# A down projection with its operands changed over: tokens held, weights moving

## The reference, cut to what matters

```python
    h2 = rmsnorm(x, g_norm[1]) * (1 + sc2) + sh2
    u, gg = jnp.split(h2 @ w_ffn_in, 2, axis=-1)          # 1024 -> 2 x 2816
    x = x + gt2 * ((jax.nn.silu(gg) * u) @ w_ffn_out)     # 2816 -> 1024
    ...
    y_prompt = rmsnorm(xp, g_final)
    y_sample = rmsnorm(xs, g_final)
```

## Time and profile before

| | |
|---|---|
| median of 3 runs | 1036.57 us (1036.42 to 1037.43) |
| span of the profiled execution | 1034.1 us (its own time is not given apart from this; the median is 2.5 above it) |
| TensorE busy | 995.1 us, 96% |
| TensorE's weight loads busy | 914.6 us, 88% |
| VectorE, ScalarE, GpSimd busy | 521.6, 447.0, 359.7 us |
| first matmul of the down projection | 884.79 us after the span's start |

### The profile page before, as it was taken

One profiled execution on the slowest core, in us unless ns is written; L12 is line 12 of the kernel. 1 busy time (PEld: TensorE's weight loads), 2 busy tenths in 40 slices (PEclk: granted clock), 3 DMA queues, 4 the chain that ended last, 5 costly groups with the idle time before them and its releaser, 6 DMA issues.

```text
span 1034.1 us, 26814 instructions
## 1 busy us (share of the span) xinstructions
PE 995.1 (96%) x10988; PEld 914.6 (88%) x10988; DVE 521.6 (50%) x1200; ACT 447.0 (43%) x991; POOL 359.7 (35%) x318
## 2 busy tenths in 40 slices
PE   6999999999999989998899999999999999999996
PEld 4899999899998666776788999999999999999996
DVE  4500000078006666666547756888888887800003
ACT  4433323354345444554432355555555556711113
POOL 1164344342332433600252354333233342133330
PEclk9999999999999999999999999999999999999998
DMA  9986756334412000002332632232423323232212
GB/s 356 395 299 228 247 189 212 107 126 148 137 45 60 13 14 13 14 24 76 126 98 85 204 122 82 74 90 82 121 81 95 108 81 97 60 110 85 84 57 87
DMA packets 118182, 122.33 MB, mean 118 GB/s; under 512 B 5396, under 2 KB 102848, under 8 KB 115656
## 3 DMA queue, kind: packets, MB, share of 16 engines
q1 hardware_dynamic: 112864, 111.86, 33.2%
q10 hardware_dynamic: 5224, 9.10, 2.7%
HBM read 108.33 MB, written 15.23 MB: 119 GB/s over the span
## 4 chain that ended last, share of the span: by engine, by line
PE 85%; DVE 7%; ACT 4%; issue 2%; POOL 1%; ACTq 1%; DVEq 0%; POOLq 0%
PE ps L1964 60%; PE ps L2586 21%; PE ps L2328 1%; DVE s_sb L1542 1%; PE ps L2228 1%; DVE hl L1356 1%; DVE Pb L1513 1%; ACT x_sq L871 0%; POOL w_lo L685 0%; DVE XX L1523 0%; PE ps L2619 0%; POOL w_lo L839 0%; ACTq L857 0%; DVE rbx L1369 0%; PE ps L2115 0%
## 5 line engine op out<-in xcount | busy, mean ns | idle before, releaser
L1964 PE MATMUL ps<-hh,w_hi 128*128 128x274 f32 x832 | 176.1, 294 | 1.5 <-DVE hl L1356 0.7
L685 POOL TENSOR_TENSOR w_lo<-w_raw,w_hi 128x2048 fp32r<-128x2048 f32 x22 | 101.4, 4607 | 213.9 <-ACT w_hi L881 197.2
L1964 PE MATMUL ps<-hl,w_hi 128*128 128x274 f32 x832 | 172.9, 290 | 1.0 <-DVE al L1878 1.0
L1964 PE MATMUL ps<-hh,w_lo 128*128 128x274 f32 x832 | 173.2, 290 | 0.0
L1964 PEld LDWEIGHTS ps<-hh,w_hi 128*128 128x128 f32 x832 | 131.5, 189 | 11.7 <-issue 9.9
L1964 PEld LDWEIGHTS ps<-hl,w_hi 128*128 128x128 f32 x832 | 131.5, 189 | 1.2 <-DVE al L1878 1.2
L1964 PEld LDWEIGHTS ps<-hh,w_lo 128*128 128x128 f32 x832 | 131.6, 190 | 0.8 <-issue 0.8
L833 POOL TENSOR_TENSOR ws_lo<-w_raw,ws_hi 128x512 fp32r<-128x512 f32 x63 | 80.6, 1294 | 144.8 <-DVE ps L1796 130.3
L2586 PE MATMUL ps<-th,ws_hi 128*128 128x274 f32 x336 | 97.5, 290 | 0.0
L2586 PE MATMUL ps<-tl,ws_hi 128*128 128x274 f32 x336 | 97.4, 290 | 0.0
L2586 PE MATMUL ps<-th,ws_lo 128*128 128x274 f32 x336 | 97.1, 289 | 0.0
(11 more groups left out here) (438 smaller groups left out, 2288.0 us busy)
## 6 DMA issues: line engine op xcount, KB each, us to landing
w_raw<-in_w_ffn_in SPq DMA_DIRECT2D x44, 512.0 KB, 4.5
w_raw<-in_w_in SPq DMA_DIRECT2D x42, 512.0 KB, 5.0
ada_l<-in_w_ada SPq DMA_DIRECT2D x16, 1024.0 KB, 6.6
ada_w<-in_w_ada SPq DMA_DIRECT2D x8, 1024.0 KB, 13.4
w_raw<-in_w_ffn_out SPq DMA_DIRECT2D x16, 384.0 KB, 3.9
w_raw<-in_w_ffn_out SPq DMA_DIRECT2D x16, 320.0 KB, 3.2
g_d<-gst SPq DMA_DIRECT2D x16, 274.0 KB, 2.2
gring<-g_d SPq DMA_DIRECT2D x16, 274.0 KB, 3.2
```

What stands on the lines that cost most here:

```text
L685: pool.tensor_tensor(w_lo[:, s, 0:cols], w_raw[:, s, 0:cols], w_hi[:, s, 0:cols].bitcast(F32), ALU.subtract).then_inc(lo_done, 1)
L1964: return pe.matmul(out, lhsT, rhs, start=start, stop=stop)
```

## The change

The down projection changes its operands over. What is held in the array is now a 128x128 block of activations (128 tokens of one channel block), and 512 columns of `w_ffn_out` move past it. The result comes out with tokens on the partitions. There are two halves of 512 output channels (`q`), each of six units: five of 4 weight blocks and one of 2 (`down_unit`), a weight block being 128 rows by 512 columns. In each half the four prompt tiles have a PSUM bank each (`DN_BANK`).

The 32 sample tokens are not in these matmuls. At the head of each unit `sample_unit` multiplies them in plain float32 with the raw weights: 32 columns held, 512 moving, the unit's (up to) four blocks side by side in four column strips of bank 1. At the end of a half, ScalarE copies the bank (`sample_copied`) and a float32 matmul with four stacked identities (`fold`) adds the four strips up (`folded`).

The residual, still in `xT`, is turned to token rows during the first five units (`turn`, 8 transposes each) and copied by ScalarE to `y_sb` (`x_rows`). Since tokens are now on the partitions, `gt2` is needed as rows: it is transposed together with the shift outputs, stored, and read back as a broadcast (`gt_row`, `gt_row_s`). VectorE's `added` multiplies a PSUM bank with this row and adds it to `y_sb`; the squares are taken for each half, and the norm is then made in place. The splits of the activations cover the 512 prompt columns only; the sample's activations go to `a_s`.

```diff
+        KG = 4
+        NGR = -(-FT // KG)
+        NDN = 2 * NGR
...
+        DN_BANK = ((4, 5, 6, 7), (0, 2, 3, 4))
+        ROWS_BANK, FOLD_BANK = 1, (5, 6)
+        Y_ORDER = (0, 1, 4, 2, 3)
...
             for j in range(2):
                 sp.wait_ge(wsum_done, WSUM + NSM * (NST - 1 + j))
                 sp.wait_ge(wslo_done, WSLO + NPL * (NST - 1 + j))
-                down_load(0, j)
...
+                down_load(j)
+            sp.wait_ge(quad_ev, QUAD + 8 + 4 * NST)
+            sp.wait_ge(ss_mm, KD)
+            sp.wait_ge(gt_out, GT_OUT + 16)
+            sp.dma_start(gt_row[:, :], gt_d[0:1, :].to_broadcast([P, D])).then_inc(gt_in, 16)
+            sp.dma_start(gt_row_s[:, :], gt_d[1:2, :].to_broadcast([TS, D])).then_inc(gt_in, 16)
+            for j in range(2, NDN):
+                sp.wait_ge(lo_done, DN0 + j - 1)
+                sp.wait_ge(rows_mm, ROWS_MM + j - 1)
+                down_load(j)
...
+            for t in range(KS):
+                down_high(2 + t)
+                x_rows(t)
+            sample_copied(0)
+            down_high(KS + 2)
+            for t in range(TT):
+                squares_of(t, 0, t)
+            down_high(KS + 3)
+            squares_of(TT, 0, TT)
+            for j in range(KS + 4, NDN):
+                down_high(j)
+            sample_copied(1)
...
+            def added(t, q, n):
...
+                link(tt(src, src, g[0:rows_, q * 512:(q + 1) * 512], ALU.mult))
+                tt(y, src, y, ALU.add).then_inc(y_added, 1)
...
+            added(0, 1, KS)
+            added(1, 1, KS + 1)
+            inverse(0, 0)
+            added(4, 1, KS + 2)
+            normed(0, 0)
+            inverse(1, 1)
+            normed(1, 1)
+            inverse(4, 2)
+            normed(4, 2)
+            added(2, 1, KS + 3)
+            inverse(2, 3)
+            normed(2, 3)
+            added(3, 1, KS + 4)
+            inverse(3, 4)
+            normed(3, 4)
...
+            def sample_unit(j):
...
+                for b in range(n):
+                    ins = mm(ps[TS * b:TS * b + TS, ROWS_BANK, :], a_s[:, k0 + b, :], w_raw[:, s, b * 512:(b + 1) * 512],
+                             k0 == 0, k0 + b + KG >= FT)
+                ins.then_inc(rows_mm, 1)
...
+            def tile_part(j, t, b0=0, b1=KG):
...
+                    for i, (x_, w) in enumerate(((x, w_hi), (xl, w_hi), (x, w_lo))):
+                        ins = mm(ps[:, DN_BANK[q][t], :], x_, w[:, j % 2, c], k == 0 and i == 0, k == FT - 1 and i == 2)
...
+            for j in range(NDN - 2):
+                q, k0, n, _ = down_unit(j)
+                if j == 1:
+                    pe.wait_ge(lo_done, DN0 + 2)
+                sample_unit(j)
+                if j == NGR:
+                    pe.wait_ge(x_turned, X_TURNED + KS)
...
+                if j < KS:
+                    turn(j)
+                if j == NGR:
+                    pe.wait_ge(ffa_f32, FFA + NST + 1)
+                    folded(0)
+            for j in range(NDN - 2, NDN):
+                sample_unit(j)
+                pe.wait_ge(lo_done, DN0 + j + 1)
+                for t in range(2):
+                    ins = tile_part(j, t)
+                    if j == NDN - 1:
+                        ins.then_inc(half_mm, 1)
+            folded(1)
+            for t in range(2, TT):
+                tile_part(NDN - 2, t)
+                tile_part(NDN - 1, t).then_inc(half_mm, 1)
```

More of the change, by code:

```diff
@@ L642, in _ @@
                 sp.wait_ge(wslo_done, WSLO + NPL * (NST - 1 + j))
-                down_load(0, j)
[L644 to L654, removed]
+                down_load(j)
[8 more added lines that the diff above has]
+                down_load(j)
+            for n, t in enumerate(Y_ORDER):
+                sp.wait_ge(yt_done, n + 1)
                 dst = y_prompt[0, t * P:(t + 1) * P, :] if t < TT else y_sample[0]
-                sp.dma_start(dst, y_sb[t][0:rows, :]).then_inc(y_out[t % 2], 16)
+                sp.dma_start(dst, y_sb[t][0:TILES[t][1], :]).then_inc(y_out[n % 2], 16)
             for q in range(2):
@@ L1291, in root @@
                 act.activation(c, c, ACT.Sqrt).then_inc(yr, 1)
[L1292 to L1301, removed]
+            for t in range(KS):
[10 more added lines that the diff above has]
+            sample_copied(1)
+            squares_of(0, 1, KS)
+            squares_of(1, 1, KS + 1)
+            root(0, 0)
+            squares_of(4, 1, KS + 2)
+            root(1, 1)
+            root(4, 2)
+            squares_of(2, 1, KS + 3)
+            root(2, 3)
+            squares_of(3, 1, KS + 4)
             root(3, 4)
-            act.wait_ge(yr, YR + 5)
-            act.wait_ge(y_first, Y_FIRST + 3)
-            act.activation(y_sb[3][:, :], y_sb[3][:, :], ACT.Copy, scale=stat[:, 3:4]).then_inc(y_by_act, 1)
         @block.vector
@@ L1922, in normed @@
                 dve.wait_ge(yr, YR + n + 1)
[L1923 to L1946, removed]
@@ L1957, in _ @@
-            scaled_by_g(3, D - P, D).then_inc(y_first, 1)
-            normed(4, 3)
+                y = y_sb[t][0:rows_, :]
+                stt(y, y, stat[0:rows_, t:t + 1], gf_row[0:rows_, :], ALU.mult, ALU.mult).then_inc(yt_done, 1)
+            dve.wait_ge(gt_in, GT_IN + 32)
+            for t in range(KS):
+                added(t, 0, t)
+            for t in range(KS):
+                first_mean(t)
+            dve.wait_ge(gf_in, GF_IN + 16)
+            added(0, 1, KS)
+            added(1, 1, KS + 1)
@@ L2613, in _ @@
-            down_tile(KD - 2, 0)
-            def turn(t, k0, k1):
-                c0, rows_ = TILES[t]
-                for k in range(k0, k1):
-                    ins = pe.transpose(ps[0:rows_, 2 * Y_PAIR[t] + k // 4, (k % 4) * P:(k % 4 + 1) * P],
-                                       xT[:, k, c0:c0 + rows_], ident[:, :])
-                return ins
-            u, n = U_DN - NST + 2 * KD - 2, T_DN + KD - 1
-            pe.wait_ge(lo_done, u + 1)
-            product(n, 1, 0, down_terms(0), True, False).then_inc(unit_mm, 1)
@@ L2645, in _, with turn @@
-            pe.wait_ge(x_last, 2)
-            pe.wait_ge(y_first, Y_FIRST + 1)
-            turn(2, KD - 1, KD).then_inc(yt_mm, 1)
-            pe.wait_ge(ysq_done, KS)
-            turn(4, KD - 1, KD).then_inc(yt_mm, 1)
-            pe.wait_ge(y_first, Y_FIRST + 2)
-            turn(3, KD - 1, KD).then_inc(yt_mm, 1)
+            def turn(t):
+                c0, rows_ = TILES[t]
+                if t:
+                    pe.wait_ge(x_turned, X_TURNED + t)
+                else:
+                    pe.wait_ge(quad_ev, QUAD + 8 + 4 * NST)
+                for k in range(KD):
+                    ins = pe.transpose(ps[0:rows_, 2 + k // 4, (k % 4) * P:(k % 4 + 1) * P], xT[:, k, c0:c0 + rows_], ident[:, :])
+                ins.then_inc(yt_mm, 1)
```

233 lines of the change are left out of this document (122 added, 111 removed).

## The result

The change made the kernel slower: 1040.68 us against 1036.78 in 7 runs of each, a ratio of 1.0036 with a 95% interval of 1.0025 to 1.0047, or some 3.7 us (2.6 to 4.9). The forecast was 3.3 us faster.

A forecast was written before the change was run, and what follows sets the result against it. TensorE's stream from the first down matmul bounds the kernel: 884.79 plus 124.8 to tile 0's completion, plus VectorE's 17.4, gives 1027.2 against 1030.42. Span 3.3 us shorter, 1030.8, plus 2.5 carried over: 1033.3 us, range 1029.5 to 1041.

The forecast's parts named there:

- Prompt matmuls: Down projection: 528 matmuls of 512 columns at 0.216 us replace 1056, 114.0 us against 134.6.
- the long records: Float32 matmuls with `ones`, two passes in one record: 548 column-times in 0.2315 us, scaled to 0.216 at 512.
- rival 1: Excess belongs to every float32r matmul: kept once each, 1038.9, or growing with columns, 1044.0; chance 22 in 100, two thirds first.
- tile 0's completion: Second half's first prompt tile complete at 1009.8 us; VectorE's line of five tiles then takes 17.4 us to the end.
- the break-even: Price of a 512-column prompt matmul from which rival 1 decides: 0.223 us.
- Strip unit: Sample rows at each unit's head: two float32 passes of 0.43 us plus 0.32, 1.18 us; 12 units 14.2.
- switching: Going into strip mode and out at each sample unit: 0.32 us.
- the early side: Wider shift transpose, copy and small store near 284 us lie beside TensorE's stream and cost nothing.
- The tail behind TensorE: From TensorE's end to the end of VectorE's last arithmetic: grows from 5.2 to 7.2 us.
- the cover: Weight split during TensorE's previous unit: 7.3 us against 6.5 at unit 6; if gone, about a us once.
- Rival 2: Strips cost more than in the adaLN product, switching doubled: +4.2 us, 1037.5; chance 8 in 100.
- rivals 3 and 4: 3: strip switching hides, 1029.1, or tail stays 5.2, 1031.3, chance 7; 4: 512-column matmuls at 0.131 each, 992, chance 1.

The follow-up runs named there:

- combined run: Changed kernel with strips of two units paired, the end in tile order and the sample fold earlier; 1035.94 us, ratio 0.9994 to the kernel before.

## Why the prediction was wrong

**The step that failed** is "Prompt matmuls": "I take 0.216: the long records have the same weight load and lose nothing to it, so the excess at 274 columns looks like a weight load that a short matmul does not quite cover". The long records were plain float32, and the excess is a property of float32r which those rows could not show. The term is 0.232, between the two forms of rival 1. Of the 0.016 that were missing, 0.011 are what float32r costs by itself over the forecast's price (0.227); the other 0.005 appear only in the kernel, and their cause stays open. For the 486 matmuls ahead of tile 0's completion it makes 486 x 0.016 = 7.8 us, where the break-even stood at 0.223. With it the forecast of the stretch, 1027.2 - 884.79 = 142.4, becomes 150.2, against 149.66 measured. Rival 1 happened, and I gave it 22 in 100. The total would read 1033.3 + 7.8 = 1041.1, against 1040.68; that this is closer still is luck, since the down projection began 1.5 us later in this profile, the last store took 3.0 us and not 3.7, and the run's time was 1.7 over its span and not 2.5. The stated range, 1029.5 to 1041, holds 1040.68 only by its upper end; the forecast's own range of 1031 to 1036 does not.

**The rest of the sum held.** Strip unit 1.18 forecast, 1.19 measured; switching 0.32 a visit, 0.31 measured; turns 0.89, 0.87; the early side nothing, nothing. From tile 0's completion to the end 17.4 was forecast and 1035.95 - 1018.65 = 17.3 measured. The tail behind TensorE is 6.4 and not 7.2, mostly because TensorE itself took longer for the work behind tile 0. No new wait of TensorE opened; at unit 6 the cover was as thin as stated, which the run without strips shows. Rival 2 (dearer switching) and rivals 3 and 4 fell. The last fell with the 131 ns that the Trainium skill gives for 512 columns in "TensorE: Matmul & The Clock Gate", Back-to-back issue gap: no type tried here comes under 0.216 at 512 columns.

**Where the gain went.** The prompt's stream by the change is 528 x 0.232 = 122.5 us. Before, 1056 matmuls took 134.6 for prompt, sample and padding together, so the stream got 12.1 us shorter, not 20.6. Most of that is not the wider move: 1056 x 274 - 528 x 512 = 19008 columns fewer, the sample's and the padding, are 7.9 us at 2.4 GHz. Fewer and wider matmuls saved the other 4.2, since 1056 excesses of 13 ns became 528 of 19; the forecast had 12.7 there. Strips and folds cost more than all of it: TensorE's 142.86 less 122.5 and 4.4 for the turns leaves them 16.0, of which 12 x 1.19 = 14.3 are the strips and 1.7 the two folds (2.4 forecast; one of them stands right behind a strip unit and shares its visit). So the sample's rows, whose columns and padding took 7.9 us in the stream, cost 16.0 outside it. With 0.3 more of turns and 1.4 less of small waits TensorE ends up 2.7 us longer, and VectorE's order at the end costs 1.2 more. The second part and some of the first were mendable, which the combined run shows: its loss is gone, with no gain left over.

**Open:** why float32r costs 11 to 13 ns more than bfloat16, and why in the kernel the excess leans on the width. No run has strips in float32r, where three products would stand in place of the four passes of plain float32.

## What to carry to other kernels

A price for a shape the trace does not have must come from the same operand type, or stand in the forecast as a range: here 16 ns on one matmul turned a forecast of 3.3 us faster into 3.7 slower. When a wider move replaces two narrow ones, write the gain as two terms: the columns that leave the stream (here 7.9 us) and the fixed part per instruction (here 4.2). Then set the first against what the rows that no longer fit the shape cost in their own form (here 16.0). At the end of a kernel put the tiles of the engine that finishes them on a clock: its time per tile against the time between deliveries, and its lag at the first tile, which is carried to the last but for the difference of the two clocks.

## What the runs showed of the hardware

- Back to back at the full clock a float32r matmul starts 0.227 us after the one before for 512 columns, 0.130 for 274 and 0.120 for 256; bfloat16 0.216, 0.117 and 0.109; plain float32 0.429 for 512 columns in each of its two records. bfloat16 and plain float32 are 2.5 ns over their columns at 2.4 GHz, float32r 13 to 16.
- In this kernel the same float32r distances are 0.232, 0.1275 and 0.118; neither the other engines nor DMA make the difference.
- float32r has a floor of 0.112 us from 224 columns down when 128 are held.
- Neither zeros, nor holding and moving the same operands, nor one bank in place of four changed the float32r price; holding 64 columns instead of 128 took 3 ns off at 274 and added 3 at 512.
- Four float32 column strips of 32 held columns run at the price of one matmul, 0.430 us for one record of each at 512 columns, and a visit to the strip form costs 0.31 us.
- The first float32r matmul of 512 columns behind small float32 ones is followed by the second only after 0.335 us. With bfloat16 it is 0.227.
